# A hybrid attention kernel: small work moved from VectorE and ScalarE to GpSimd, remainders in four pieces

## The reference, cut to what matters

```python
h = rmsnorm(x, norm_g)
(a_q, a_k, a_v, a_z, i_q, i_k, i_w, b_q, b_k, b_v, b_z, b_o, b_i, b_f, g_a, g_b) = split(h @ w_in)
o_a = dsa_attention(rope(a_q), rope(a_k), a_v, rope(i_q), rope(i_k), i_w * 16 ** -0.5, 128)
y_a = (o_a * silu(a_z)) @ w_branch_a
q_b, k_b = split(silu(causal_conv(concat(b_q, b_k), conv_w, conv_b)))
cell = mlstm_chunkwise(q_b, k_b * 128 ** -0.5, b_v, b_i + b_igate, log_sigmoid(b_f + b_fgate))
h_b = head_norm(sigmoid(b_o) * cell, head_norm_g)       # (y - mean) * rsqrt(var + eps) over a head
y_b = (h_b * silu(b_z)) @ w_branch_b
merged = sigmoid(g_a) * y_a + sigmoid(g_b) * y_b
out = rmsnorm(x + merged @ w_out, final_norm_g)
```

## Time and profile before

| | |
|---|---|
| median of three runs | 523.63 us |
| the profiled execution's own time | 523.32 us |
| its span | 521.6 us |
| TensorE busy | 501.7 us, 96% |
| VectorE busy | 266.9 us, 51% |
| ScalarE busy | 241.1 us, 46% |
| GpSimd busy | 196.0 us, 38% |
| mean granted TensorE clock | 0.994 |

### The profile page before, as it was taken

How to read it: one execution, slowest core, us unless ns; L and a number is a source line. 1 busy time by engine, 2 the same in 40 slices (tenths; PEclk the granted TensorE clock), 3 DMA queues, 4 the chain that set the end, 5 groups by cost and what they waited for, 6 DMA issues and landing times.

```text
span 521.6 us, 6712 instructions
## 1 busy us (share of the span) xinstructions
PE 501.7 (96%) x2480; PEld 418.9 (80%) x2480; DVE 266.9 (51%) x577; ACT 241.1 (46%) x422; POOL 196.0 (38%) x112
## 2 busy tenths in 40 slices
PE   3999999999999999998989999999999999999995
PEld 3688888888888877886878888888888888887885
DVE  3675777877999925419756686321110111125333
ACT  7856755655444245346675655153313333152322
POOL 0775231423444443245322222154346643473000
PEclk9999999999999999999999999999999999999998
DMA  8653431222233341122113031140344327443112
GB/s 280 173 155 121 148 93 40 82 82 82 80 86 117 103 120 41 41 82 73 50 40 79 3 82 41 40 121 24 99 121 122 80 64 220 122 128 153 42 40 82
DMA packets 44841, 48.94 MB, mean 94 GB/s; under 512 B 4996, under 2 KB 29700, under 8 KB 44808
## 3 DMA queue, kind: packets, MB, share of 16 engines
q1 hardware_dynamic: 43944, 47.39, 30.8%
q10 hardware_dynamic: 864, 1.12, 0.6%
HBM read 46.40 MB, written 2.11 MB: 93 GB/s over the span
## 4 chain that ended last, share of the span: by engine, by line
PE 87%; ACT 4%; DVE 3%; issue 2%; POOL 2%; DMA 1%; POOLq 0%; ACTq 0%; DVEq 0%
PE pj L1368 21%; PE pj L1370 21%; PE pj L1369 21%; PE ob L1472 3%; PE tr L1466 2%; PE ob L1446 2%; PE qb L1436 2%; PE qb L1431 2%; PE qb L1430 2%; POOL w_lo L501 2%; PE ob L1370 1%; PE ob L1368 1%; PE qb L1370 1%; PE qb L1368 1%; PE ob L1369 1%
## 5 line engine op out<-in xcount | busy, mean ns | idle before, releaser
L501 POOL TENSOR_TENSOR w_lo<-w_raw,w_hi 128x1024 fp32r<-128x1024 f32 x71 | 171.0, 2419 | 171.0 <-ACT w_hi L794 171.0
L1368 PE MATMUL pj<-w_hi,h_hi 128*128 128x512 f32 x272 | 113.1, 416 | 0.0
L1370 PE MATMUL pj<-w_hi,h_lo 128*128 128x512 f32 x272 | 107.0, 393 | 0.0
L1369 PE MATMUL pj<-w_lo,h_hi 128*128 128x512 f32 x272 | 107.0, 393 | 0.0
L1368 PE MATMUL pj<-h_hi,w_hi 128*128 128x512 f32 (+1 forms) x200 | 78.2, 391 | 1.7 <-DVE h_lo L1025 1.7
L794 ACT ACTIVATE w_hi<-w_raw 128x1024 fp32r<-128x1024 f32 (+1 forms) x74 | 75.7, 1046 | 8.7 <-DMA w_raw<-in_w_out 6.1
L1370 PE MATMUL pj<-h_hi,w_lo 128*128 128x512 f32 (+1 forms) x200 | 77.9, 389 | 0.0
L1369 PE MATMUL pj<-h_lo,w_hi 128*128 128x512 f32 (+1 forms) x200 | 77.8, 389 | 0.0
L1370 PEld LDWEIGHTS pj<-w_hi,h_lo 128*128 128x128 f32 x272 | 51.3, 189 | 11.5
L1368 PEld LDWEIGHTS pj<-w_hi,h_hi 128*128 128x128 f32 x272 | 51.3, 189 | 9.6 <-issue 1.0
L1369 PEld LDWEIGHTS pj<-w_lo,h_hi 128*128 128x128 f32 x272 | 51.5, 189 | 9.4 <-issue 1.0
(11 more groups left out here) (192 smaller groups left out, 829.6 us busy)
## 6 DMA issues: line engine op xcount, KB each, us to landing
w_raw<-in_w_in SPq DMA_DIRECT2D x60, 512.0 KB, 3.6
w_raw<-in_w_out SPq DMA_DIRECT2D x5, 512.0 KB, 3.6
x_tok<-in_x SPq DMA_DIRECT2D x4, 512.0 KB, 5.1
w_raw<-in_w_branch_a SPq DMA_DIRECT2D x8, 256.0 KB, 3.0
w_raw<-in_w_branch_b SPq DMA_DIRECT2D x8, 256.0 KB, 3.3
x_again<-in_x SPq DMA_DIRECT2D x1, 2048.0 KB, 8.5
w_late<-in_w_out SPq DMA_DIRECT2D x3, 512.0 KB, 6.5
neg_m_all<-neg_m_d SPq DMA_DIRECT2D x4, 256.0 KB, 4.6
```

Of the source, the lines that this page charges most:

```text
L501: eng.tensor_tensor(lo[:, 0:m], raw_slot(n)[:, 0:m], hi[:, 0:m].bitcast(F32), ALU.subtract).then_inc(lo_by_dve if n in DVE_SLOTS else lo_b ...
L1368: pe.matmul(bank, a_hi, b_hi, start=first, stop=False)
L1369: pe.matmul(bank, a_hi, b_lo, start=False, stop=False)
L1370: return pe.matmul(bank, a_lo, b_hi, start=False, stop=last)
```

## The change

- **Newton steps.** GpSimd gets `inverse_root`: variance plus epsilon, a first guess from the bits of the number, three Newton steps, then the shift: 17 instructions on 128 x 16 values, each waiting for the one before. It runs after GpSimd's remainder in bz's first unit. ScalarE's square root and VectorE's reciprocal and shift are gone.
- **Query remainders.** The two subtractions for q_lo per tile go from VectorE to GpSimd, at the same places.
- **Query ring moved.** `q_twice` and `q_lo` lie in the zone of `qk_b`, which is free after the last `qk_b` job. Tile 0 is split at the first quarter of bo, four places earlier; the zeroing too. `oa` and `ob` exchange zones, and `w_last` goes with `oa`.
- **Output gate in its bank.** tanh of bo is written back to its PSUM bank; VectorE adds one and scales there, then multiplies by the cell. The bank is released by that product, no longer by tanh, and ScalarE no longer waits for VectorE before the next tanh.
- **Gated product on GpSimd.** The product of bz with the cell goes from VectorE to GpSimd, at the start of the next unit, ahead of its remainder. The one semaphore of gated products becomes two.
- **First slots.** GpSimd rounds slots 1 and 2 itself and makes their remainders; ScalarE rounds slot 3 after the last h_hi tile, and VectorE makes its remainder after the last h_lo tile; slot 4 as before.
- **Remainders in four pieces.** Every remainder on GpSimd is four instructions of 256 columns. Waits count pieces.
- **Warm-up.** 13 matmuls on the zero mask run on TensorE before the constants arrive.

The diff, cut to its core:

```diff
+POOL_ROUNDS = (1, 2)
+WARM = 13
-DVE_SLOTS = (0, OUT0 + 2, OUT0 + 4, OUT0 + 6, OUT0 + 7)
+DVE_SLOTS = (0, 3, OUT0 + 2, OUT0 + 4, OUT0 + 6, OUT0 + 7)
+PIECES = 4
-SPLIT_AT = {attn_place(A_HEADS * i - 6) if i else attn_place(-3): i for i in range(TILES)}
+SPLIT_AT = {attn_place(A_HEADS * i - 6) if i else first_quarter("bo"): i for i in range(TILES)}
...
-        oa_hi = at("oa_hi", [P, KW, SEQ], F32R, z_a)
+        oa_hi = at("oa_hi", [P, KW, SEQ], F32R, z_f)
-        q_twice = at("q_twice", [P, 2, 2, A_HEADS // 2, P], F32R, z_a)
+        q_twice = at("q_twice", [P, 2, 2, A_HEADS // 2, P], F32R, z_f)
-        ob_hi = at("ob_hi", [P, KW, SEQ], F32R, z_f)
+        ob_hi = at("ob_hi", [P, KW, SEQ], F32R, z_a)
...
+            for a in range(0, m, m // PIECES):
+                cols = slice(a, a + m // PIECES)
+                eng.tensor_tensor(lo[:, cols], raw_slot(n)[:, cols], hi[:, cols].bitcast(F32), ALU.subtract)\
+                    .then_inc(lo_by_pool, 1)
...
             elif UNITS[u][0] == "bo":
-                eng.wait_ge(gate_t_made, UNITS[u][1] + 1)
+                eng.wait_ge(bo_scaled, UNITS[u][1] + 1)
...
-                if p == first_quarter("bo") + 4:
-                    wait_full(pool, ("pv_b", B_HEADS - 1, TILES - 1))
+                if p == first_quarter("bo"):
+                    wait_full(pool, ("qk_b", B_HEADS - 1, TILES - 1))
...
+                if p in SPLIT_AT:
+                    i = SPLIT_AT[p]
+                    for e in range(2):
+                        same = slice(e * A_DIM, (e + 1) * A_DIM)
+                        pool.wait_ge(q_hi_made, 2 * i + e + 1)
+                        hi = q_twice[same, i % 2, e, :, :]
+                        pool.tensor_tensor(q_lo[same, i % 2, e, :, :], q_a[same, :, i * P:(i + 1) * P],
+                                           hi.bitcast(F32), ALU.subtract).then_inc(q_lo_made, 1)
+                        pool.wait_ge(q_lo_made, 2 * i + e + 1)
...
             for n in range(N_SMALL_SLOTS, N_SMALL_SLOTS + 4):
-                remainder(pool, n)
+                if n in POOL_ROUNDS:
+                    pool.wait_ge(raw_in[raw_place(n)], raw_count(n))
+                    pool.tensor_copy(split_slot(n)[0], raw_slot(n)).then_inc(hi_by_pool, 1)
+                if n not in DVE_SLOTS:
+                    remainder(pool, n)
+            def inverse_root():
+                pool.wait_ge(b_var_made, TILES)
+                mean, var = mean_var[:, :, :, 0], mean_var[:, :, :, 1]
+                r, half, t = b_rstd[:, :, :], b_mean_neg[:, :, :], root_t[:, :, :]
+                bits = r.bitcast(I32)
+                step(pool.tensor_scalar(r, var, 4 * EPS, None, ALU.add))
+                step(pool.tensor_scalar(half, r, -0.5, None, ALU.mult))
+                step(pool.tensor_scalar(bits, bits, -0.5, float(ROOT_SEED), ALU.mult, ALU.add))
+                for _ in range(3):
+                    step(pool.tensor_tensor(t, r, r, ALU.mult))
+                    step(pool.tensor_tensor(t, t, half, ALU.mult))
+                    step(pool.tensor_scalar(t, t, 1.5, None, ALU.add))
+                    step(pool.tensor_tensor(r, r, t, ALU.mult))
+                step(pool.tensor_scalar(t, mean, -1.0, None, ALU.mult))
+                pool.tensor_tensor(half, t, r, ALU.mult).then_inc(b_shift, 1)
+            def gated_cell(j):
+                ring = gated[:, j % 2, :].rearrange("p (h d) -> p h d", d=B_DIM)
+                pool.wait_ge(zg_scaled, j + 1)
+                pool.wait_ge(b_normed, j + 1)
+                pool.tensor_tensor(ring, ring, cell[:, j, :, 0:B_DIM], ALU.mult).then_inc(gated_b_made, 1)
...
-                if k in (1, 4, 7):
-                    round_slot(1 + k // 3)
+            round_slot(3)
             round_slot(4)
...
-                if (g, j) == ("bz", 0):
-                    act.wait_ge(b_var_made, TILES)
-                    act.activation(b_rstd[:, :, :], mean_var[:, :, :, 1], ACT.Sqrt, bias=eps_col[:, 1:2])\
-                        .then_inc(b_root, 1)
...
+            remainder(dve, 3)
...
-                    link(dve.tensor_tensor(c, c, den[:, j, :].unsqueeze(2).to_broadcast([P, B_HEADS, B_DIM]), ALU.mult))
-                    ins = dve.scalar_tensor_tensor(out=c, in0=gate_ring[j % 2][:, :].rearrange("p (h d) -> p h d", d=B_DIM),
-                                                   scalar=1.0, in1=c, op0=ALU.add, op1=ALU.mult)
+                    gate = pj[u % 2][:, :].rearrange("p (h d) -> p h d", d=B_DIM)
+                    link(dve.scalar_tensor_tensor(out=gate, in0=gate, scalar=1.0,
+                                                  in1=den[:, j, :].unsqueeze(2).to_broadcast([P, B_HEADS, B_DIM]),
+                                                  op0=ALU.add, op1=ALU.mult))
+                    dve.tensor_tensor(c, gate, c, ALU.mult).then_inc(bo_scaled, 1)
...
+            pe.wait_ge(pool_step, 2)
+            for _ in range(WARM):
+                pe.matmul(pj[1][:, 0:P], mask0, mask0, start=True, stop=True)
```

More of the change, by code:

```diff
@@ L23 @@
 F32R = mybir.dt.float32r
+I32 = mybir.dt.int32
 P = 128
@@ L210 @@
 MASKED = -1.0e30
+ROOT_SEED = 0x5F3759DF
 def hybrid_kernel(nc, x, norm_g, w_in, conv_w, conv_b, b_igate, b_fgate, head_norm_g,
@@ L494, in wait_lo @@
             else:
-                eng.wait_ge(lo_by_pool, sum(1 for m in range(n + 1) if m not in DVE_SLOTS))
+                eng.wait_ge(lo_by_pool, PIECES * sum(1 for m in range(n + 1) if m not in DVE_SLOTS))
         def remainder(eng, n):
-            eng.wait_ge(hi_made, n + 1)
+            if n in POOL_ROUNDS:
+                eng.wait_ge(hi_by_pool, POOL_ROUNDS.index(n) + 1)
+            else:
+                eng.wait_ge(hi_made, sum(1 for m in range(n + 1) if m not in POOL_ROUNDS))
             m = slot_size(n)
             hi, lo = split_slot(n)
-            eng.tensor_tensor(lo[:, 0:m], raw_slot(n)[:, 0:m], hi[:, 0:m].bitcast(F32), ALU.subtract).then_inc(lo_by_dve if n in DVE_SLOTS else lo_by_pool, 1)
+            if n in DVE_SLOTS:
+                eng.tensor_tensor(lo[:, 0:m], raw_slot(n)[:, 0:m], hi[:, 0:m].bitcast(F32), ALU.subtract)\
+                    .then_inc(lo_by_dve, 1)
+                return
+            for a in range(0, m, m // PIECES):
+                cols = slice(a, a + m // PIECES)
+                eng.tensor_tensor(lo[:, cols], raw_slot(n)[:, cols], hi[:, cols].bitcast(F32), ALU.subtract)\
+                    .then_inc(lo_by_pool, 1)
         def slot_size(n):
@@ L701, in _, with step @@
         def _(pool):
+            steps = [2]
+            def step(ins):
+                steps[0] += 1
+                ins.then_inc(pool_step, 1)
+                pool.wait_ge(pool_step, steps[0])
             pool.memset(one_col[:, :], 1.0)
@@ L706, in _ @@
             pool.wait_ge(pool_step, 1)
-            pool.memset(mask0[0:CHUNK, CHUNK:P], MASKED)
+            pool.memset(mask0[0:CHUNK, CHUNK:P], MASKED).then_inc(pool_step, 1)
             def side(p):
-                if p == first_quarter("bo") + 4:
-                    wait_full(pool, ("pv_b", B_HEADS - 1, TILES - 1))
-                    pool.wait_ge(lo_by_pool, sum(1 for m in range(group_slot("bz") + 2) if m not in DVE_SLOTS))
+                if p == first_quarter("bo"):
+                    wait_full(pool, ("qk_b", B_HEADS - 1, TILES - 1))
+                    pool.wait_ge(lo_by_pool, PIECES * sum(1 for m in range(group_slot("bz") + 1) if m not in DVE_SLOTS))
                     for e in range(2):
@@ L1212, in job_side @@
                         .then_inc(o_lo, 1)
-            def split_queries(i):
-                for e in range(2):
-                    same = slice(e * A_DIM, (e + 1) * A_DIM)
-                    dve.wait_ge(q_hi_made, 2 * i + e + 1)
-                    hi = q_twice[same, i % 2, e, :, :]
-                    dve.tensor_tensor(q_lo[same, i % 2, e, :, :], q_a[same, :, i * P:(i + 1) * P], hi.bitcast(F32),
-                                      ALU.subtract).then_inc(q_lo_made, 1)
             def cell_scale():
@@ L1284, in unit_rest @@
                     dve.wait_ge(b_var_made, j + 1)
-                elif g == "bz":
-                    ring = gated[:, j % 2, :].rearrange("p (h d) -> p h d", d=B_DIM)
-                    dve.wait_ge(zg_scaled, j + 1)
-                    dve.wait_ge(b_normed, j + 1)
-                    dve.tensor_tensor(ring, ring, cell[:, j, :, 0:B_DIM], ALU.mult).then_inc(gated_made, 1)
                 elif g == "az":
@@ L1312, in _ @@
                 if c == KT - 1:
-                    for n in DVE_SLOTS[1:3]:
+                    for n in DVE_SLOTS[2:4]:
                         remainder(dve, n)
@@ L1474, in side @@
                 elif kind in ("out_a_chan", "out_b_chan"):
-                    pe.wait_ge(gated_made, OUT_ORDER.index(job) + 1)
+                    pe.wait_ge(gated_a_made if kind == "out_a_chan" else gated_b_made, job[1] + 1)
                     ring = gated[:, OUT_ORDER.index(job) % 2, :]
```

43 lines of the change are left out of this document (20 added, 23 removed).

## The result

Four executions of the changed kernel took 516.15 to 516.41 us, median 516.3; four of the kernel before on the same chip 523.12 to 523.88, median 523.42. The ratio is 0.9862, with a 95% interval of 0.9849 to 0.9874: 7.1 us faster. The forecast was 515.5 us, so the result is 0.8 us above it and inside the forecast's range.

What follows compares the result with a forecast made beforehand. TensorE was taken as the bound, busy 501.7 of 521.6 us, so only its idle time and slow stretches could be won. Attention -6.9, first slots -0.4 and end -0.7 sum to -8.0: 515.5 us, range 513.5 to 518.7.

Steps and rivals of the forecast that it cites:

- Attention, -6.9: Attention stretch: five TensorE waits, 5.2 us in all, and the lowered clock, 1.7, go; bounds -6.9 to -6.0.
- The long wait with its clock: TensorE's 2.23 us wait ending at 272.41 and the lowered clock right after it, 1.7 us, both counted in full.
- q_lo's wait: TensorE's wait for q_lo before the first qk_a, 0.8 us as shown, removed by the change.
- The later ones: Other attention waits for exponentials and probs_t, after VectorE's q_lo at 243.8 and 284.4 and a gated product: gone.
- The root chain, 4.3 us: GpSimd's 17 small instructions at 0.25 us each, done at 264.9 (263.7 to 266.5), needed by 266.6.
- rival A: The root's chain, or what follows it, is later than 266.6; at worst 519.6 us; chance 0.12.
- First slots, -0.4: Start: slot 1's remainder done at 16.0 instead of 16.36, so small_chan and the start come 0.4 us earlier.
- C: Time of GpSimd's copy that rounds slot 1 at the start: taken as 1.1 us, bounds 0.95 and 2.35.
- Rival B: GpSimd's copy costs as much as its subtraction: start +1.9 in place of -0.4, 517.8 us; chance 0.14.
- Remainders in pieces elsewhere: 0.: Some 70 slots outside the start and end: pieces cost 0.4 us more per slot, but covered, so no change.
- The end, -0.7: Last product: m_lo some 1.0 us earlier, against a load held up by up to 0.9; ends -1.4 and +0.5.
- Rival C: Pieces don't let VectorE in, since the next is queued already: end 0, 516.2 us; chance 0.10.

## Why the prediction was right, and where it was off

- **Attention, -6.9: measured -7.2.** All five waits went, and the clock with them. The long wait with its clock gave 4.00 (4.1 forecast), 2.42 by the wait and 1.58 by the clock; with the root alone it was 4.0 in the kernel before, and 3.5 came back when the root was undone. q_lo's wait gave 0.88 (0.96). The later ones gave 2.34 (1.85). Most of the 0.5 between is a sixth wait that the sum of five left out, since the list of the earlier trace rows shows none so short: in the kernel before the product with the values at 246.80 starts 0.12 after TensorE's last matmul is drawn to end, and TensorE gained 0.36 there. The rest is that the three others cost 0.17 to 0.25 more each than shown, not 0.16.
- **The root chain, 4.3 us: measured 5.3.** The step was mis-sized, 0.31 in place of 0.25: the gap between two dependent instructions is 0.08, where I took the 0.05 of the memsets, and the instruction itself 0.22 to 0.25. It stayed under the upper bound of 0.34 and under the cover. The forecast of the whole wait rested on this cover, and it was 0.9 us in the changed kernel and 0.5 in the kernel before with the root alone; rival A was that near.
- **Which edit removed the later waits.** I credited the q_lo pair and the gate product together. The runs show that q_lo on GpSimd or the pieces removed 2.3, either of them. Undone alone, beside pieces and with q_lo on GpSimd, the gate in its bank gave nothing and the product on GpSimd 0.35; what they would give without the pieces was not run. That the pieces answer the same wait stood in the prediction, as a rule beside the VectorE term, but not that either of the two is enough.
- **First slots, -0.4: measured -0.43.** C was 1.11 and the remainder was done at 15.89: the term as said. Its reading of the earlier trace rows was not quite right: at 21.41 only the weight load waits. The matmul before starts at 21.29 and the transposes at 21.52, one step of 0.23 later, so in the kernel before TensorE's own work and small_chan came together. The change moved TensorE's own work by 1.1 (21.29 to 20.18, near the 1.2 that the prediction has for it), so small_chan alone decides afterwards, and TensorE waits 0.50 for it. Had it moved by less than 0.43, the start would have gained less. Rival B did not happen.
- **"Remainders in pieces elsewhere: 0."** Right between 30 and 450 us: whole remainders were 0.45 ahead at 21 us, 0.72 at 225 and 0.74 through attention. The 0.45 are slot 1's pieces, which stood in the term of the first slots (2.77 for 2.41); the 0.3 behind them I had counted at nothing.
- **The end, -0.7: measured +0.53. This is the one term that failed, sign and all**: "In pieces DVE waits for one piece: some 1.0 earlier for m_lo." DVE did wait for one piece (0.96 saved), but I set against it "up to 0.9" for a late load and then took -0.7 all the same. The load was fully late, 0.99. And I left out that pieces run later too: OUT0 + 5 took 3.81 us with VectorE in between, which lengthened the last sum by 0.52 and made TensorE wait 0.38 for w_lo. The value lay at the end of the range that I had kept (+0.5), and the total came out inside its range because this term is small beside the rest. Rival C, no entry between pieces, is refuted by the 1.62.
- **Sum.** -7.22 - 0.43 + 0.53 = -7.12, and the span went from 521.6 to 514.5. The forecast of 515.5 was 0.8 too low: +1.2 from the end, -0.3 from attention, and -0.1 from carrying it to a median.

The Trainium skill, "SBUF — State Buffer", Who interferes with whom, has the exclusion for a whole instruction between a VectorE instruction with two SBUF inputs and a GpSimd one that reads SBUF. The trace agrees both ways: 2.58 to 1.62 where GpSimd's instruction got shorter, 0.69 to 1.21 where a piece stood in the way of a sum that used to run free.
